# A third place for split weights, modulation loads of the wide projections dealt into two halves, gathers shared by two engines

## The chip, the cores and the metric

The kernel runs on one core of one Trainium2 chip. The engines are TensorE (PE, matrix products; PEld is its weight load), VectorE (DVE), ScalarE (ACT), GpSimd (POOL) and SyncE (SP), whose queue issues the DMA loads. All run on their own and are tied by semaphores; each does its instructions in strict order. The metric is the time of one execution in microseconds (us), lower is better.

## The reference

Two blocks of a network run over 256 tokens of width 2048, all in float32. The part that fixes the work, cut:

```python
def first_block(...):
    h = rmsnorm(x); proj = h @ w_in                 # 2048 x 5120
    x = x + concat([pool_mixer(u), hgrn2(q, f, i, g)]) @ w_out
    x = x + memory_cross_attention(h, m, wq, wk, wv, wo)   # four 2048 x 2048
    x = x + hierarchical_moe(h, ...)                # 16 experts, width 512, top 1 group, top 2 in it
...
def second_block(x, c, ...):
    c_act = jax.nn.silu(c)
    for l in range(2):
        mod = c_act @ w_ada[l] + b_ada[l]           # 2048 x 6144
        shift, scale, gate = jnp.split(mod, 3, axis=-1)
        h = _rmsnorm(x, norm_g[l]) * (1.0 + scale) + shift
        z = h @ w_in[l]                             # 2048 x 6656, 13 pieces
        o_fft = _fourier_mix(f_x, w_fft[l]) * silu(f_g)
        o_na = _neighbourhood_attention(na_q, na_k, na_v, ...) * silu(na_g)
        o_ret = _retention(r_q, r_k, r_v, ...) * silu(r_g)
        o_cv = _conformer_conv(cv_a, cv_b, ..., w_pw[l]) * silu(cv_g)
        x = x + gate * (concat([o_fft, o_na, o_ret, o_cv]) @ w_out[l])
```

## The kernel before, in words

**Weight blocks.** All large weights are read in blocks of 128 x 2048 float32 (1 MB). SyncE loads each into a raw room (`load`, L471); the rooms are dealt by `raw_rooms`: four outside the experts, more in them. ACT writes 256 times the block as float16 (`w_hi`, L644), DVE what is left over, raw times 256 minus the high half (`w_lo`, L1292, in `split`), and thereby gives the room back (`raw_taken`). There are two places for the halves (`SPL`), so ACT's work on a block waits until PE is done with the block two back (`block_done`). PE makes 48 products of a block (`product`, L2241): high weights with high and low activations, low weights with the high ones. It waits for the split of its own block (`taken`).

**Stages.** `w_in` (40 blocks), `w_out`, `wk`, `wq`, `wv`, `wo` (16 each), `moe` (192 blocks in a larger ring), then for each layer `z0`/`z1` (the wide projection, 52 blocks) and `mix0`/`mix1` (16). In the experts, tokens are first gathered by matmuls into 16 pieces (L2556, L2670 follows); ACT evicts the high half of each (`gather_hi`), DVE the low half (`gather_lo`, L1867).

**Modulation.** The product with `w_ada` (12 units of 16 steps) is done on the side. A step is a load of 0.5 MB (`load_ada`, L476) into one of two staging halves and one operation on DVE, sum plus weights times a column (`ada_step`, L1263), which stands right behind the split of its block. `ada_plan` lists the block of each step. SyncE issues the load of block m, then the modulation loads of block m - 2 (`load_due(2)`), and each of these waits until the step two back is done (`ada_used`). A unit ends with small products on PE (`ada_columns`) and an addition (`ada_add`). Units 7 and 8 run in z0, 10 and 11 in z1, all in blocks 2 to 29, with staging and sums in `Z` (`Z_UNITS`).

**Beside the wide projection.** Its 13 pieces come in `Z_ORDER`; attention, retention, Fourier mixing and convolution are written between blocks at fixed numbers. `TAPS_AT` deals the 124 taps of the convolution to blocks. After block 43 SyncE loads `w_fft` into a raw room, after block 48 `conv_w_pw`. The room of `w_fft` is given back by PE itself, at the last product of `fft_map` (L2818), which stands ahead of block 45. DVE has `conv_norm` (L2068 to L2071) and `mixed_lo` (L2124) between the splits of blocks 44 and 45.

The order of all this is written out by hand in each engine's program; no scheduler changes it.

Of the kernel before, what the change touches and what calls it, by code (L numbers as in the profile page):

```python
# [24 lines left out]
SPL = 2  # L25
# [24 lines left out]
Z_UNITS = (7, 8, 10, 11)  # L50
# [4 lines left out]
TAPS_AT = {**{m: 4 for m in range(11, 20)}, 20: 6, 21: 3, 22: 5, 23: 6, 24: 3, 25: 5, 26: 6, 27: 3, 28: 3, 29: 6, 30: 2,  # L55
           31: 6, 32: 2, 33: 6, 34: 3, 35: 4, 36: 4, 37: 4, 38: 7}
# [140 lines left out]
def build(nc, A, table, const_at, columns, router, out):  # L197
    ctx = ExitStack()
    with ctx:
# [21 lines left out]
        w_hi = sb("w_hi", [P, SPL, BLK], F16)  # L221
        w_lo = sb("w_lo", [P, SPL, BLK], F16)
# [65 lines left out]
        f_parts = w2[:, 0:1024].rearrange("p (a k g n) -> p a k g n", a=TT, k=2, g=4)  # L288
        f_last = w2[:, 1024:1032].rearrange("p (a g) -> p a g", a=TT)
# [8 lines left out]
        LO_AT = {"ga": 0, "weight": KC, "t": KC + 1, "y": KC + 1 + 4 * TILES}  # L298
# [77 lines left out]
        def ada_bank(u):  # L376
            return MB[:, 0, 0:8] if u in (8, 11) else GB[:, 2, 0:8]
# [77 lines left out]
        def _(sp):  # L455
# [26 lines left out]
            def load_due(depth):

                while len(due) > depth:
# [136 lines left out]
        def _(act):  # L621
            def split_half(ph, j, half):
# [7 lines left out]
                act.activation(w_hi[:, s % SPL, cut], raw_at[r][:, cut], ACT.Copy, scale=W_SCALE).then_inc(hi_done, 1)  # L630

            def split(ph, j, i=0):
# [3 lines left out]
                if ph == "moe":  # L636
                    act.wait_ge(block_done[s % SPL], s // SPL - 1)
# [375 lines left out]
            for n in range(MOE_STEPS):  # L1013
                f, last = n // 8, n % 8 == 7
                for part in range(2):
# [19 lines left out]
                    if n == 2 and part == 1:  # L1035
# [205 lines left out]
        def _(dve):  # L1241
# [23 lines left out]
            def ada_add(u):  # L1265
                dve.wait_ge(ada_mm, u + 1)
                mod = MOD[:, u // 6, u % 6 * 8:u % 6 * 8 + 8]
                if u % 6 < 4:
# [5 lines left out]
                    ("z0", 20): 7, ("z0", 33): 8, ("mix0", 14): 9, ("z1", 20): 10, ("z1", 33): 11}  # L1274

            def split_half(ph, j, half):
# [1717 lines left out]
```

## Time and profile before

| | us |
|---|---|
| median of three runs | 2095.44 |
| lowest, highest | 2094.69, 2101.43 |
| profiled execution | 2093.71 |
| its span | 2091.7 |
| outside the span | 2.0 |

The mean clock granted to PE is 0.994 of full. The stages in the profiled execution, by PE's work: w_in to 265.5, w_out to 353.2, wk to 439.6, wq to 533.8, wv to 629.7, wo to 724.7, experts 738 to 1233, z0 1248.5 to 1572.8, mix0 to 1660.1, z1 1668.0 to 1994.0, mix1 to 2077.7. Times in the timelines are counted from the span's start. The waits view adds up the idle time of an engine under what ended it, so a wait for several things stands under the last one.

### The profile page before, as it was taken

How to read it: one execution, taken by the hardware profiler on the slowest of the kernel's cores; microseconds unless marked ns; L12 is line 12 of the kernel's file. 1: busy time of each engine (PE TensorE's matmuls, PEld its weight loads, DVE VectorE, ACT ScalarE, POOL GpSimd, SP SyncE). 2: the span in 40 equal slices, each digit the busy share in tenths (PEclk: the TensorE clock that was granted, in tenths of full speed). 3: DMA queues.
4: the chain of work that ended last, by engine and by line, in shares of the span. 5: the costliest groups of instructions: out<-in, count | busy, mean ns of one | idle time of the engine just before them, and what ended most of it. 6: DMA issues, size and time to landing. Idle time of an engine off the chain costs nothing.

```text
span 2091.7 us, 42599 instructions
## 1 busy us (share of the span) xinstructions
PE 2041.4 (98%) x18993; PEld 1641.1 (78%) x18993; DVE 1752.3 (84%) x1670; ACT 1194.1 (57%) x1071; POOL 41.3 (2%) x40
## 2 busy tenths in 40 slices
PE   8999999999999989999999999999999899999998
PEld 7889888888889946555556568888888788888887
DVE  7875787988888799999999999999668779996555
ACT  5554644444445478877877864456554444565543
POOL 0002300000000000000000000000000000000000
PEclk9999999999999999999999999999999999999999
DMA  8854487789888878999999987874458778744452
GB/s 303 317 202 162 163 314 271 280 307 326 319 326 298 309 280 355 420 420 420 420 420 416 408 318 293 294 256 164 143 184 310 281 286 304 250 162 159 181 202 101
DMA packets 95717, 593.23 MB, mean 284 GB/s; under 512 B 10664, under 2 KB 10824, under 8 KB 36784
## 3 DMA queue, kind: packets, MB, share of 16 engines
q1 hardware_dynamic: 94912, 583.73, 74.4%
q0 software_dynamic: 624, 6.80, 0.8%
q8 instruction: 149, 2.44, 0.5%
q14 instruction: 32, 0.26, 0.0%
HBM read 588.39 MB, written 2.10 MB: 282 GB/s over the span
## 4 chain that ended last, share of the span: by engine, by line
PE 68%; DVE 16%; DMA 10%; ACT 3%; issue 3%; DVEq 0%; SPq 0%; POOL 0%; ACTq 0%; POOLq 0%
PE GB L2241 52%; DVE w_lo L1292 6%; PE GB L2670 4%; DVE W L1292 3%; PE MB L2670 3%; DMA raw<-w_up 3%; DMA W<-w_ada 2%; ACT w_hi L644 2%; DMA Z<-w_ada 2%; DMA raw<-w_down 2%; DVE W L1263 1%; DVE Z L1263 1%; DMA raw<-w_gate 1%; PE MB L2839 1%; PE MB L2441 1%
## 5 line engine op out<-in xcount | busy, mean ns | idle before, releaser
L644 ACT ACTIVATE w_hi<-raw 128x2048 f16<-128x2048 f32 x308 | 588.1, 1910 | 705.5 <-PE GB L2241 680.9
L1292 DVE SCALAR_TENSOR_TENSOR w_lo<-raw,w_hi 128x2048 f16<-128x2048 f32 x308 | 706.0, 2294 | 244.9 <-ACT w_hi L644 244.2
L2241 PE MATMUL GB<-H,w_hi 128*128 128x256 f16 x4352 | 718.9, 273 | 18.3 <-DVE w_lo L1292 11.6
L2241 PE MATMUL GB<-H,w_lo 128*128 128x256 f16 x2176 | 593.8, 273 | 0.0
L2241 PEld LDWEIGHTS GB<-H,w_hi 128*128 128x128 f16 x4352 | 421.6, 98 | 85.0 <-DVE w_lo L1292 16.6
L2241 PEld LDWEIGHTS GB<-H,w_lo 128*128 128x128 f16 x2176 | 213.2, 98 | 24.9
L2241 PE MATMUL GB<-w_hi,H 128*128 128x256 f16 x1280 | 210.7, 273 | 0.0
L1263 DVE SCALAR_TENSOR_TENSOR W<-W,SM 128x1024 f32<-128x1024 f32 x120 | 153.8, 1282 | 31.8 <-DMA W<-w_ada 28.5
L2241 PE MATMUL GB<-w_lo,H 128*128 128x256 f16 x640 | 174.4, 273 | 0.0
L2241 PE MATMUL GB<-Z,w_hi 128*128 128x256 f16 x1024 | 170.0, 274 | 2.9 <-DVE w_lo L1292 2.9
L2241 PE MATMUL GB<-W,w_hi 128*128 128x256 f16 x1024 | 168.0, 273 | 2.7 <-DVE w_lo L1292 2.7
L2241 PE MATMUL GB<-Z,w_lo 128*128 128x256 f16 x512 | 140.4, 274 | 0.0
L2241 PE MATMUL GB<-W,w_lo 128*128 128x256 f16 x512 | 139.6, 273 | 0.0
L2241 PEld LDWEIGHTS GB<-w_hi,H 128*128 128x128 f16 x1280 | 124.7, 98 | 16.1 <-issue 1.3
L1292 DVE SCALAR_TENSOR_TENSOR W<-raw,W 128x2048 f16<-128x2048 f32 x54 | 123.2, 2286 | 2.3 <-ACT W L644 2.2
L644 ACT ACTIVATE W<-raw 128x2048 f16<-128x2048 f32 x54 | 103.0, 1911 | 20.9 <-DMA raw<-w_down 6.1
L2241 PEld LDWEIGHTS GB<-Z,w_hi 128*128 128x128 f16 x1024 | 100.4, 98 | 16.0 <-DVE w_lo L1292 3.8
L2241 PEld LDWEIGHTS GB<-W,w_hi 128*128 128x128 f16 x1024 | 99.9, 98 | 14.9 <-DVE w_lo L1292 3.3
L2008 DVE SCALAR_TENSOR_TENSOR Y<-Y,PC 128x256 f32<-128x256 f32 x240 | 99.6, 479 | 0.0
L2670 PE MATMUL GB<-W,Z 128*64 (+1 forms) x864 | 86.7, 353 | 4.4 <-DVE Z L1867 4.3
L2670 PE MATMUL MB<-W,Z 128*64 (+1 forms) x864 | 86.0, 353 | 1.3 <-DVE W L1292 1.2
L1263 DVE SCALAR_TENSOR_TENSOR Z<-Z,SM 128x1024 f32<-128x1024 f32 x60 | 76.8, 1281 | 10.7 <-DMA Z<-w_ada 9.9
(489 smaller groups left out, 2789.9 us busy)
## 6 DMA issues: line engine op xcount, KB each, us to landing
raw<-w_in SPq DMA_DIRECT2D x144, 1024.0 KB, 5.2
W<-w_ada SPq DMA_DIRECT2D x128, 512.0 KB, 5.6
raw<-w_out SPq DMA_DIRECT2D x48, 1024.0 KB, 5.1
raw<-w_down SPq DMA_DIRECT2D x41, 1024.0 KB, 10.6
raw<-w_gate SPq DMA_DIRECT2D x34, 1024.0 KB, 11.0
raw<-w_up SPq DMA_DIRECT2D x32, 1024.0 KB, 12.8
Z<-w_ada SPq DMA_DIRECT2D x64, 512.0 KB, 5.9
raw<-xattn_wk SPq DMA_DIRECT2D x16, 1024.0 KB, 5.1
```

What stands on the lines that cost most here:

```text
L644: act.activation(w, raw_at[r], ACT.Copy, scale=W_SCALE).then_inc(hi_done, 1)
L1263: dve.scalar_tensor_tensor(sums, w, SM[:, 24 + k:25 + k], sums, ALU.mult, ALU.add).then_inc(ada_used[n % 2], 1)
L1292: dve.scalar_tensor_tensor(lo, raw_at[r], W_SCALE, hi, ALU.mult, ALU.subtract).then_inc(raw_taken[r], 1)
L2008: dve.scalar_tensor_tensor(ca[:, c, :], CU[:, c, k // 4:k // 4 + T], col("conv_w_2", l * TAPS * 4 + k), ca[:, c, :], ALU.mult, ALU.add).th ...
L2241: last = pe.matmul(o, a, m, start=first, stop=end and w_part is lo, skip_group_check=True)
L2441: ins = pe.matmul(MB[:, h % 2, a * T:a * T + T], x_q[q][:, 4 * h + c, a * P:a * P + P], x_k[k][:, 4 * h + c, :], start=a == 0 and c == 0 a ...
L2670: ins = pe.matmul(o_bank(j, k)[r:r + SLOT], x[:, c0 + c, at_:at_ + SLOT], v, start=kh == 0 and c == 0 and part == 0, stop=kh == 7 and c == ...
L2839: ins = pe.matmul(banks[:, n // 2, n % 2 * T:n % 2 * T + T], w[:, k, n * P:n * P + P], x[:, k, :], start=n % 2 == 0 and k == 0, stop=k == ...
```

## The change

- `SPL` is 3. Two places stay as they were; the third is the fourth raw room, cut into a high and a low half (`third`, `hi_of`, `lo_of`). Block s uses place `(s + 2) % 3`. ACT waits for the block three back.
- Three raw rooms are left outside the experts; the fourth joins the ring there from the experts' fifth block, and the wide projection gets it back as a place.
- The gathers' low half of odd pieces goes from DVE to ACT.
- `ada_plan`: in z0 and z1 the first unit stands in blocks 2 to 16, the second in blocks 35 to 46 and is staged in `W` instead of `Z`; its first load waits for the attention's output (`na_o`, `LATE_ROOM`). Its columns are at block 50, its addition at 51.
- `TAPS_AT` deals the same 124 taps anew. `f_parts` and `f_last` move from `w2` to `w1`. In the experts the router's steps, `best_two`, `place_rows` and an exponential stand one to three steps later.

```diff
-SPL = 2
+SPL = 3
-Z_UNITS = (7, 8, 10, 11)
+Z_UNITS = (7, 10)
...
-TAPS_AT = {**{m: 4 for m in range(11, 20)}, 20: 6, 21: 3, 22: 5, 23: 6, 24: 3, 25: 5, 26: 6, 27: 3, 28: 3, 29: 6, 30: 2,
-           31: 6, 32: 2, 33: 6, 34: 3, 35: 4, 36: 4, 37: 4, 38: 7}
+TAPS_AT = {11: 5, 12: 4, 13: 6, 14: 4, 15: 6, 16: 4, 17: 6, 18: 6, 19: 6, 20: 6, 21: 6, 22: 2, 23: 6, 24: 6, 25: 2, 26: 6, 27: 6, 28: 2, 29: 4, 30: 6, 32: 6, 33: 2, 34: 6, 35: 2, 36: 3, 37: 2}
...
-        open_ = list(range(RAW))
+        open_ = list(range(RAW - 1))
         if 0 <= j < n:
-            open_ += [4] * (j >= 6) + [5] * (7 <= j < 126) + [6] * (j >= 7) + [7] * (13 <= j < 150)
+            open_ += [3] * (j >= 4) + [4] * (j >= 6) + [5] * (7 <= j < 126) + [6] * (j >= 7) + [7] * (13 <= j < 150)
...
-    def fast(ph):
-        for m in [2 + 2 * k // 3 for k in range(13)] + list(range(11, 30)):
+    def halves(ph):
+        for m in [2, 2, 3, 4, 4, 5, 6, 6, 7, 8, 8, 9, 10, 12, 14, 16]:
+            put(ph, m)
+        for m in [35, 36, 37, 37, 38, 39, 39, 40, 41, 41, 42, 42, 43, 44, 45, 46]:
             put(ph, m)
...
+        third = raw[:, RAW - 1, :].bitcast(F16)
+        hi_of = [w_hi[:, 0, :], w_hi[:, 1, :], third[:, 0:BLK]]
+        lo_of = [w_lo[:, 0, :], w_lo[:, 1, :], third[:, BLK:2 * BLK]]
+
+        def slot(s):
+
+            return (s + 2) % SPL
...
-                    act.wait_ge(block_done[s % SPL], s // SPL + 2 * i)
-                    w = w_hi[:, s % SPL, :]
+                    act.wait_ge(block_done[s % SPL], s // SPL)
+                    if (ph, j) == ("z0", 0):
+                        given_up(act, RAW - 1)
+                    w = hi_of[slot(s)]
...
             def gather_hi(c):
                 act.wait_ge(S("moe_mm"), MM_AT["ga"] + c + 1)
+                if c % 2:
+                    act.activation(xs_lo[:, c, :], gather_bank(c, 1), ACT.Copy)
...
             def gather_lo(c):
-                dve.wait_ge(S("moe_mm"), MM_AT["ga"] + c + 1)
-                dve.tensor_copy(xs_lo[:, c, :], gather_bank(c, 1)).then_inc(S("moe_lo"), 1)
+                if c % 2 == 0:
+                    dve.wait_ge(S("moe_mm"), MM_AT["ga"] + c + 1)
+                    dve.tensor_copy(xs_lo[:, c, :], gather_bank(c, 1)).then_inc(S("moe_lo"), 1)
...
-                    if m == 17:
+                    if m == 19:
                         ada_columns(7 + 3 * l)
-                    if m == 32:
-                        pe.wait_ge(S("na_max"), 8 * l + 8)
+                    if m == 50:
+                        pe.wait_ge(S("fft_act"), 7 * l + 7)
                         ada_columns(8 + 3 * l)
```

What stands in SyncE's order in z0 around the load of `w_fft`, before. `raw_taken` with a number is the room that the load waits for, `raw<-w_in` the weight block; the last four are blocks 44, 45, 46 and 47:

```order
L471 DMA raw<-w_in 128x2048 [waits raw_taken3]
L471 DMA raw<-w_fft 128x2048 [waits raw_taken0]
L536 DMA NYQ<-w_nyq 4x512
L471 DMA raw<-w_in 128x2048 [waits raw_taken1]
L471 DMA raw<-w_in 128x2048 [waits raw_taken2]
L471 DMA raw<-w_in 128x2048 [waits raw_taken3]
L471 DMA raw<-w_in 128x2048 [waits raw_taken0]
```

Now, from the same place; the weight blocks are 44, 45, 46 and `ada_used` is the staging half that a modulation load waits for:

```order
L482 DMA raw<-w_fft 128x2048 [waits raw_taken0]
L550 DMA NYQ<-w_nyq 4x512
L482 DMA raw<-w_in 128x2048 [waits raw_taken1]
L487 DMA W<-w_ada 128x1024 [waits ada_used0]
L487 DMA W<-w_ada 128x1024 [waits ada_used1]
L482 DMA raw<-w_in 128x2048 [waits raw_taken2]
L487 DMA W<-w_ada 128x1024 [waits ada_used0]
L482 DMA raw<-w_in 128x2048 [waits raw_taken0]
L487 DMA W<-w_ada 128x1024 [waits ada_used1]
```

The room of `w_fft` is asked for again by block 46's load instead of block 47's, and two modulation loads stand ahead of block 45's, one ahead of and one behind block 46's.

DVE's order in z0 from the split of block 44, before (`hi_done` is ACT's high half, `mix_hi` its part of the mixed output):

```order
L1292 SCALAR_TENSOR_TENSOR w_lo<-raw,w_hi 128x2048 [waits hi_done]
L2068 RECIPROCAL NS<-NS 128x256 [waits conv_dve,conv_act]
L2069 TENSOR_TENSOR Y<-Y,NS 128x1024 [waits dve_step]
L2071 TENSOR_SCALAR Y<-Y,PC 128x256 [waits dve_step]
L2071 TENSOR_SCALAR Y<-Y,PC 128x256 x3
L2124 TENSOR_TENSOR W<-Y,W 128x1024 [waits mix_hi]
L1292 SCALAR_TENSOR_TENSOR w_lo<-raw,w_hi 128x2048 [waits hi_done] x2
```

Now, from the same split to the split of block 45 and the modulation step behind it:

```order
L1310 SCALAR_TENSOR_TENSOR w_lo<-raw,w_hi 128x2048 [waits hi_done]
L1281 SCALAR_TENSOR_TENSOR W<-W,SM 128x1024 [waits ada_used0,ada_full1]
L2087 RECIPROCAL NS<-NS 128x256 [waits conv_dve,conv_act]
L2088 TENSOR_TENSOR Y<-Y,NS 128x1024 [waits dve_step]
L2090 TENSOR_SCALAR Y<-Y,PC 128x256 [waits dve_step]
L2090 TENSOR_SCALAR Y<-Y,PC 128x256 x3
L2143 TENSOR_TENSOR W<-Y,W 128x1024 [waits mix_hi]
L1310 SCALAR_TENSOR_TENSOR raw<-raw 128x2048 [waits hi_done]
L1281 SCALAR_TENSOR_TENSOR W<-W,SM 128x1024 [waits ada_used1,ada_full0]
```

A modulation step stands behind each of the two splits, the first ahead of `conv_norm`, and the split of block 45 writes its low half into the fourth raw room.

## Rows read from the trace of the kernel before

**Rows 1.** The page's first part: busy us of each engine, share of the span, instructions.

```profile
PE 2041.4 (98%) x18993; PEld 1641.1 (78%) x18993; DVE 1752.3 (84%) x1670; ACT 1194.1 (57%) x1071; POOL 41.3 (2%) x40
```

**Rows 2.** Table by stage: length, busy of PE, PEld, DVE, ACT, POOL, clock, DMA share, GB/s.

```profile
738.10:1233.00 494.90, 482.89 (x4845) 274.76 (x4846) 472.66 (x297) 399.95 (x276) 0.00 (x0) 1.00 0.98 396
1248.50:1572.80 324.30, 320.26 (x2814) 274.33 (x2815) 279.43 (x345) 169.40 (x193) 0.00 (x0) 1.00 0.63 225
1668.00:1994.00 326.00, 320.35 (x2812) 273.89 (x2813) 273.28 (x329) 169.39 (x193) 0.00 (x0) 1.00 0.63 225
```

**Rows 3.** Waits of PE: engine and line, waited for what; us in total, times, longest.

```profile
PE GB L2241 <- DVE w_lo L1292: 17.3, 20, 2.1
PE GB L2670 <- DVE Z L1867: 5.2, 5, 1.6
```

**Rows 4.** The same view, waits of DVE.

```profile
DVE w_lo L1292 <- ACT w_hi L644: 246.0, 167, 9.6
DVE W L1263 <- DMA W<-w_ada: 28.5, 33, 1.8
```

**Rows 5.** Timeline of SyncE's queue in z0: start us, us, engine, line, operation, tiles.

```profile
1491.65 37.99 SPq L471 DMA_DIRECT2D raw<-w_in  x5
```

**Rows 6.** Waits of SyncE's queue, 1480 to 1540.

```profile
SPq L471 <- PE GB L2818: 22.9, 1, 22.9
```

**Rows 7.** Timeline of DVE in z0, blocks 41 to 45.

```profile
1491.55 1.22 DVE L2055 SCALAR_TENSOR_TENSOR Z<-MB,Z 128x1024 f32<-128x1024 f32 x1
...
1500.30 0.68 DVE L1995 TENSOR_TENSOR Z<-Y 128x512 f32<-128x512 f32 x1
1501.02 0.42 DVE L1996 TENSOR_TENSOR Z<-Z 128x256 f32<-128x256 f32 x1
...
1505.54 0.42 DVE L2059 COPY Z<-GB 128x256 f32<-128x256 f32 x1
...
1508.26 1.23 DVE L2102 TENSOR_TENSOR raw<-raw 128x1024 f32<-128x1024 f32 x1
1512.21 2.29 DVE L1292 SCALAR_TENSOR_TENSOR w_lo<-raw,w_hi 128x2048 f16<-128x2048 f32 x1 [2.73 <-ACT w_hi L644]
1514.42 1.75 DVE L2068 RECIPROCAL NS<-NS 128x256 f32<-128x256 f32 x1
...
1519.89 2.28 DVE L1292 SCALAR_TENSOR_TENSOR w_lo<-raw,w_hi 128x2048 f16<-128x2048 f32 x1
```

**Rows 8.** Timeline of PE in z0: retention, then the starts of blocks 43, 44, 45.

```profile
1489.62 1.08 PE L2765 MATMUL GB<-Z 128*64 128x256 f32 x8
...
1510.44 0.38 PE L2241 MATMUL GB<-H,w_hi 128*128 128x256 f16 x2
...
1515.68 0.38 PE L2241 MATMUL GB<-H,w_hi 128*128 128x256 f16 x2
...
1528.96 0.38 PE L2241 MATMUL GB<-H,w_hi 128*128 128x256 f16 x2
```

**Rows 9.** Timeline of SyncE's queue in w_out: a weight load and the modulation load behind.

```profile
300.12 0.33 SPq L471 DMA_DIRECT2D raw<-w_out  x1
300.50 0.43 SPq L476 DMA_DIRECT2D W<-w_ada  x1
```

**Rows 10.** Modulation loads (L476), 300 to 325: issue to landing.

```profile
DMA to landing us min/median/max: 5.9/6.3/6.8
```

**Rows 11.** The same line, 1390 to 1405.

```profile
DMA to landing us min/median/max: 5.2/5.3/5.4
```

**Rows 12.** The page's fifth part: busy us, mean ns, idle before; a modulation step on DVE.

```profile
L1263 DVE SCALAR_TENSOR_TENSOR W<-W,SM 128x1024 f32<-128x1024 f32 x120 | 153.8, 1282 | 31.8 <-DMA W<-w_ada 28.5
```

**Rows 13.** Table of stretches, columns as in rows 2: two blocks of w_in, and pre-experts.

```profile
38.17:45.09 6.92, 6.92 (x48) 5.49 (x49) 6.38 (x5) 1.27 (x3) 0.00 (x0) 0.75 0.99 374
45.09:50.33 5.24, 5.24 (x50) 4.70 (x48) 3.04 (x2) 2.40 (x2) 0.00 (x0) 1.00 0.98 392
728.11:734.94 6.83, 6.79 (x36) 6.08 (x35) 5.60 (x32) 3.72 (x7) 0.00 (x0) 0.50 0.87 367
```

More of the change, by code:

```diff
@@ L165, in ada_plan @@
         put("wo", m)
-    fast("z0")
+    halves("z0")
     for m in [2, 2, 3, 4, 4, 5, 6, 6, 7, 8, 8, 9, 9, 10, 10, 11]:
         put("mix0", m)
-    fast("z1")
+    halves("z1")
     assert count[0] == 12 * ADA_STEPS
@@ L220, in build @@
         raw = sb("raw", [P, RAW, BLK])
-        w_hi = sb("w_hi", [P, SPL, BLK], F16)
-        w_lo = sb("w_lo", [P, SPL, BLK], F16)
+        w_hi = sb("w_hi", [P, 2, BLK], F16)
+        w_lo = sb("w_lo", [P, 2, BLK], F16)
         XT = sb("XT", [P, KC, T])
@@ L287, in build @@
         RO = Y[:, 5:7, :]
-        f_parts = w2[:, 0:1024].rearrange("p (a k g n) -> p a k g n", a=TT, k=2, g=4)
-        f_last = w2[:, 1024:1032].rearrange("p (a g) -> p a g", a=TT)
+        f_parts = w1[:, 0:1024].rearrange("p (a k g n) -> p a k g n", a=TT, k=2, g=4)
+        f_last = w1[:, 1024:1032].rearrange("p (a g) -> p a g", a=TT)
         f_cos, f_nyq, f_sin = Zf[:, 0:2 * MIRROR], Zf[0:4, 2 * MIRROR:3 * MIRROR], Zf[:, 2 * T:2 * T + 2 * MIRROR]
@@ L297, in build @@
         HI_AT = {"ga": 0, "pt": KC, "t": KC + 3, "y": KC + 3 + 4 * TILES}
-        LO_AT = {"ga": 0, "weight": KC, "t": KC + 1, "y": KC + 1 + 4 * TILES}
+        LO_AT = {"ga": 0, "weight": KC // 2, "t": KC // 2 + 1, "y": KC // 2 + 1 + 4 * TILES}
         SQ_AT = {"x": 0, "wo": 4, "two": 12, "mix0": 18, "mix1": 26}
@@ L361, in ada_sums @@
             if u in Z_UNITS:
-                return Zf[:, (4 * (u in (8, 11))) * T:(4 * (u in (8, 11)) + 4) * T]
+                return Zf[:, 0:4 * T]
             return SUMS[:, u % 2, :]
@@ L376, in ada_bank @@
         def ada_bank(u):
-            return MB[:, 0, 0:8] if u in (8, 11) else GB[:, 2, 0:8]
+            return MB[:, 0, 0:8] if u in Z_UNITS else GB[:, 2, 0:8]
         def na_p(h):
@@ L418, in piece_end, with done @@
             return 2 + u if i == 0 and ph in K_MAJOR else 4 * i + 2 * u + 1
-        def done(eng, ph, j, i=0):
+        def done(eng, ph, j):
             s = where(ph, j)[1]
-            eng.wait_ge(block_done[s % SPL], s // SPL + 1 + 2 * i)
+            eng.wait_ge(block_done[s % SPL], s // SPL + 1)
         def pieces_in(eng, k):
@@ L464, in load @@
                     sp.wait_ge(raw_taken[r], n - 1)
+                elif r == RAW - 1:
+                    done(sp, "wo", 13)
                 elif r == 4:
@@ L478, in _ @@
             ADA_ROOM = {"w_out": ("hgrn_y", 2), "z0": ("norm_ms", 4), "mix0": ("small_mm", 2), "z1": ("norm_ms", 5)}
+            LATE_ROOM = {8 * ADA_STEPS: 4, 11 * ADA_STEPS: 8}
             due = []
@@ L488, in load_due @@
                     for step in steps:
+                        if step in LATE_ROOM:
+                            sp.wait_ge(S("na_o"), LATE_ROOM[step])
                         load_ada(step)
@@ L629, in split_half @@
                 cut = slice(half * BLK // 2, half * BLK // 2 + BLK // 2)
-                act.activation(w_hi[:, s % SPL, cut], raw_at[r][:, cut], ACT.Copy, scale=W_SCALE).then_inc(hi_done, 1)
+                act.activation(hi_of[slot(s)][:, cut], raw_at[r][:, cut], ACT.Copy, scale=W_SCALE).then_inc(hi_done, 1)
             def split(ph, j, i=0):
@@ L636, in split @@
                 if ph == "moe":
-                    act.wait_ge(block_done[s % SPL], s // SPL - 1)
+                    act.wait_ge(block_done[(s - 4) % SPL], (s - 4) // SPL + 1)
                     if j < 2:
@@ L1034, in _ @@
                             turned_hi(n // 16 - 1, k)
-                    if n == 2 and part == 1:
+                    if n == 3 and part == 1:
                         act.wait_ge(S("r_exp_in"), 1)
@@ L1273, in _ @@
             adds = {("w_in", 22): 0, ("wk", 10): 1, ("wq", 9): 2, ("wv", 3): 3, ("wv", 13): 4, ("wo", 8): 5,
-                    ("z0", 20): 7, ("z0", 33): 8, ("mix0", 14): 9, ("z1", 20): 10, ("z1", 33): 11}
+                    ("z0", 20): 7, ("z0", 51): 8, ("mix0", 14): 9, ("z1", 20): 10, ("z1", 51): 11}
             def split_half(ph, j, half):
@@ L1280, in split_half @@
                 cut = slice(half * BLK // 2, half * BLK // 2 + BLK // 2)
-                ins = dve.scalar_tensor_tensor(w_lo[:, s % SPL, cut], raw_at[rooms[b][0]][:, cut], W_SCALE, w_hi[:, s % SPL, cut], ALU.mult, ALU.subtract)
+                ins = dve.scalar_tensor_tensor(lo_of[slot(s)][:, cut], raw_at[rooms[b][0]][:, cut], W_SCALE, hi_of[slot(s)][:, cut], ALU.mult, ALU.subtract)
                 if half:
@@ L1926, in _ @@
                     if part == 1:
-                        if n == 0:
+                        if n == 2:
                             groups_left()
-                        if n == 2:
+                        if n == 3:
                             best_two()
@@ L1932, in _ @@
                             combine()
-                        if n in (3, 4):
-                            place_rows(n - 3)
+                        if n in (4, 6):
+                            place_rows(n // 2 - 2)
                     if n == 6 and part == 1:
@@ L2224, in product @@
                 s = at[ph][1] + j
-                hi = w_hi[:, s % SPL, :].rearrange("p (c n) -> p c n", c=8)
-                lo = w_lo[:, s % SPL, :].rearrange("p (c n) -> p c n", c=8)
+                hi = hi_of[slot(s)].rearrange("p (c n) -> p c n", c=8)
+                lo = lo_of[slot(s)].rearrange("p (c n) -> p c n", c=8)
                 first = start
@@ L2702, in na_scores @@
                         evicted(pe, l, 3)
+                        pe.wait_ge(ada_mod, 8 + 3 * l)
                     else:
@@ L2736, in rotate @@
                     if j == 0:
-                        pe.wait_ge(ada_mod, 8 + 3 * l)
+                        pe.wait_ge(ada_mod, 7 + 3 * l)
                     else:
```

9 lines of the change are left out of this document (4 added, 5 removed).

## The prediction

> **What bounds the kernel now.** The page's first part is read first: TensorE (PE) is busy 2041.4 of the 2091.7 us of the span [rows 1]. A change pays only where PE stands still. The table by stage says where that is [rows 2]: in z0 and z1 all but 4 to 6 us are matmuls, and only the mixture of experts (first row) is tied to DMA, at a share of 0.98. PE's waits are the second view: 17.3 us in 20 waits for the low half of a weight block (longest 2.1) and 5.2 us in the gathers, the first two lines of a list that falls off fast [rows 3]. So a third place has at most some 17 us to win outside the experts, and halved gathers about 5. Third view, VectorE's (DVE) waits: 246.0 us in 167 for the high half, 28.5 in 33 for modulation loads, the longest 1.8 [rows 4]. DVE has slack, but its order is fixed, so a late modulation load stops all that is queued behind it, splits included.
>
> **The dangerous place: w_fft.** In each wide projection SyncE loads w_fft after block 43, into a raw room of the ring. That room isn't given back by a DVE split but by PE: `fft_map`'s last matmul, ahead of block 45. Before, SyncE waited 22.9 us for it [rows 6], within the five loads that run from 1491.65 to 1529.64 [rows 5]. That was harmless: with four rooms the load that waited was that of block 47, blocks 44 to 46 were out already, and no modulation load stood behind it. The change makes it three rooms and puts steps of unit 8 there. The order of SyncE shows that now block 46's load waits for the room, and behind it, on a queue in strict order, the modulation load that DVE wants in block 44, since modulation loads are issued two blocks late. DVE has that step ahead of `conv_norm`, `mixed_lo` and the split of block 45; PE can't begin block 45 without that split. The load thus starts when PE is already idle, and three engines take turns.
>
> **Times at that place, layer 0.** First X, from the end of a split (a room comes free) to the landing of a modulation load that is queued behind the weight load. The two are issued 0.4 us apart [rows 9]; the second lands 5.9 to 6.8, median 6.3, after its issue [rows 10]. X = 0.4 + 6.3 = 6.7 us. Lower bound: elsewhere it lands 5.2 to 5.4 after its issue [rows 11], 0.4 + 5.2 = 5.6. But there it was issued 1.2 us behind the weight load and so had less ahead of it; the value of the close pairs is the nearer one. Upper bound, with the longest landing: 7.2.
>
> The Trainium skill, "DMA: Bandwidth & Descriptors", section "Anatomy of one DMA — SWDGE (gpsimd) path", gives about 2.0 us and bytes/436e9 for one transfer. For 1.5 MB that is an estimate of 5.6 us, with the 0.4 between the issues 6.0 instead of 6.7; it would take 0.7 off each of six terms, 4.2 us. It speaks of GpSimd's path, these are SyncE's, and the landings above contradict it, so the rows decide.
>
> Now the chain. DVE split block 44 at 1512.21 and block 45 at 1519.89 [rows 7]; PE reached block 43 at 1510.44 and block 44 at 1515.68, so the split of block 44 was over 1.2 us ahead, that of block 45 long before [rows 8]. In the new order block 44's load waits for the split of block 42, with the two modulation loads of block 42 behind it. DVE's three operations on retention's first scores (from 1491.55, 2.7 us) can begin when PE has these at 1490.6 [rows 8]; the split of block 42, 2.3, follows them: 1495.6, if its load is there. Then:
> - the first of the two lands at 1495.6 + 6.7 = 1502.3, the second 1.3 later; a step takes 1.28 us [rows 12], so both are over at 1504.9. With 1.1 for the convolution's squares (0.68 and 0.42, rows 7) and the split (2.29), block 43 is ready at 1508.3. PE wants it at 1510.44: no wait.
> - block 45's load waits for this split, the next modulation load lands at 1508.3 + 6.7 = 1515.0, its step ends at 1516.3. Then come the copy and the three tensor operations that stood at 1505.54 to 1509.45 (3.9), and the split (2.3): block 44 is ready at 1522.5. PE wants it at 1515.68: **wait of 6.9 us**.
> - PE does block 44 and `fft_map`, whose last matmul before the change ended at about 1528.9, and block 45 started at 1528.96, a wait of under 0.1 [rows 8]. Call that end T0. Now T0 + 6.7 is the landing, + 1.3 the step, + 5.5 `conv_norm` and `mixed_lo` (1514.42 to 1519.89, rows 7), + 2.3 the split = T0 + 15.8: **wait of 15.7 us**.
>
> Nothing covers these: PE has the 24 matmuls of `fft_map` and nothing else ahead of block 45. Together 22.6 us a layer. Layer 1 has the same order and almost the same figures (320.35 against 320.26 us of matmuls [rows 2]), so **+45.2 us**. Bounds: with X at 5.6, 3.3 less a layer (it enters three times), so −6.6; at 7.2, 0.5 six times, +3.0.
>
> **The clock.** After a wait of some 2 us that ended at 38.17 (one of those in rows 3), the granted clock of PE is 0.75 on average over a block, which takes 6.92 us, the next 5.24 at 1.00 [rows 13]: 1.7 us. The levels are 1.2 and 2.4 GHz, so it was at the lower for about half. After a longer pause ahead of the experts it was 0.50 for all of 6.83 us, which costs 3.4. Four long waits at 1.7 each: **+6.8** (bounds 0, if no fall follows, and 13.6).
>
> **The gathers.** ScalarE (ACT) takes the low half of odd pieces, DVE half as many copies; PE's waits there are 5.2 us [rows 3]. In this stretch ACT has time. The experts then run with DMA, which is full behind them: what the gathers give comes through only as far as loads were not the limit. I take **−4** (bounds −5 and 0).
>
> **The third place and the halves.** ACT's split no longer waits for the block two back but three back. Gain: part of the 17.3 us, at most −9, since those waits at the start of w_in (2.1 among them) are loads and norm work that a place doesn't make earlier. Loss: one raw room fewer means that load and modulation loads are released one block later. Two consecutive blocks with three steps between them need of DVE's chain X + 1.3 + 1.3 + 2.3 = 11.6 us, against 10.5 for PE's two blocks; there are 14 such pairs (4 in w_in, 3 in z0, 4 in mix0, 3 in z1), each up to 1.1 us less the lead built up, at most +12. I take **0** net, the middle of −9 and +12. The convolution's taps dealt into other blocks are the same instructions: the busiest blocks now have 6 and no step, as some had before; cover is DVE's own wait for the high half [rows 4]. 0. The steps of unit 8, which leave blocks 11 to 29, relieve SyncE and DVE where PE didn't wait anyway. In the experts, `groups_left`, `best_two`, the exponential and `place_rows` come one to two steps later, work of a few us in total whose reader, the gathers, is far off: 0. `ada_columns` of unit 8 at block 51 is 16 small matmuls as before: 0.
>
> **Sum.** 2093.7 (profiled execution, 2.0 us above its span) + 45.2 + 6.8 − 4 + 0 = 2141.7. The median of the runs is 1.7 above the profiled execution: **2143 us**, 2.3% slower.
>
> **Rivals.**
> - **The lead covers it (faster).** One mechanism: at w_fft the modulation load of block 44 is out before `fft_map` ends. It decides if the load is issued 15.8 us ahead of T0. Then the waits of the low half (17.3), some of them, and of the gathers go, and DVE has freer blocks 11 to 29: −20, about 2075. For it: DVE waits 246 us on ACT, so slack is plenty [rows 4]. Against: the printed order leaves SyncE no way past the room's release. Chance 0.03.
> - **Only the weight load is late.** If DVE had its step of block 44 from elsewhere, block 46 alone hangs on T0: landing 4.8, ACT 1.9, DVE 2.3 are 9.0, against 5.24 of block 45, wait 3.7. Twice, with 3.4 for the clock and −4 for the gathers: 2095.4 + 7.4 + 3.4 − 4 = 2102. It is also what remains if DVE's work between is overlapped by something that I overlook. Chance 0.05.
> - **Pairs with three steps fall behind too.** The deficits of the 14 pairs open in full, +12: 2155. For it: DVE waited already 28.5 us for such loads with a room more [rows 4]. Chance 0.15.
> - **It doesn't do what it says** (PE reaches block 44 later than thought, by waits earlier in the stage, so that its wait of 6.9 shrinks; the sum moves along with the last rival). It's inside the forecast's range.
>
> **How the numbers follow.** The forecast has 0.77. Low end: no clock loss −6.8, X at its lower bound −6.6, and 7.6 of the 9 that the places may gain: 2122. High end: clock +6.8, X +3.0, pairs +11: 2164. This leaves out the two cheap rivals (0.08) and some tail. A measurement of this kernel can tell 0.3%, 6.3 us, from no change; the forecast and the third rival are slower beyond it (0.92), the second rival (+6.6) lies at the bound and I split it evenly, 0.025 and 0.025. Faster 0.03, same 0.03, slower 0.94.
>
> **What would show it.** In the changed kernel: a wait of SyncE for `fft_map` that now has block 46's load behind it; DVE's longest waits for a modulation load (over 5 us) right after the split of blocks 43 and 44; two PE waits for a low half in each of z0 and z1, near 7 and 16 us, the second directly behind `fft_map`; a granted clock of 0.50 after them; PE's waits in the gathers near 0. A wait of under 4 us behind `fft_map` would make the forecast wrong, and a wait for modulation loads in w_in or mix0 of over 1 us a block would speak for the third rival.

## The result and the profile after

The changed kernel takes 2205.52 us (median of 4, 2202.47 to 2207.54) against 2095.07 before: a ratio of 1.0519, 95% interval 1.0495 to 1.0543. The forecast was 2143 us, slower by 2.3%; it is slower by 5.2%, and outside the range of 2122 to 2164. The direction and one mechanism were right, the size wasn't.

The page's first part of the changed kernel, which answers to rows 1:

```profile
span 2205.7 us, 42602 instructions
PE 2066.4 (94%) x18993; PEld 1647.7 (75%) x18993; DVE 1751.9 (79%) x1662; ACT 1196.7 (54%) x1079; POOL 42.4 (2%) x40
```

The work is the same: DVE is busy 1751.9 us, before 1752.3. PE's busy time grew by 25 of the 114 us, with the same instructions at a lower granted clock (0.977 on average, before 0.994); the rest is PE standing still. For what, its list of waits says (changed kernel; us in total, times, longest):

```profile
PE GB L2260 <- DVE w_lo L1310: 76.3, 41, 15.1
PE GB L2260 <- DVE raw L1310: 28.9, 14, 16.0
PE MB L2689 <- DVE W L1310: 4.0, 4, 2.1
```

Both first lines are the low half of a weight block (`raw` is the third place, cut from the fourth raw room): 105 us in 55 waits, where rows 3 had 17.3 in 20. DVE in turn waits for modulation loads, where rows 4 had 28.5 in 33 (and the same list 9.9 in 9 for those in `Z`):

```profile
DVE W L1281 <- DMA W<-w_ada: 203.3, 86, 22.7
DVE w_lo L1310 <- ACT w_hi L660: 82.2, 61, 6.8
DVE Z L1281 <- DMA Z<-w_ada: 31.2, 20, 3.3
DVE raw L1310 <- ACT raw L660: 23.6, 12, 9.0
```

DVE's waits for the high half fell from 246.0 to 82.2 + 23.6 us, and reappear as waits for loads of `w_ada`. A table of stages, worked out from PE's first and last product of each stage in the traces, tells where the time went (us longer than before; one profiled execution of each kernel; "w_in to wo" is the sum of its six stages; "w_fft" is from the start of block 42 to that of block 47, both layers together, and is taken out of z0 and z1):

| kernel | w_in to wo | experts | z0 + z1 without w_fft | w_fft | mix0 |
|---|---|---|---|---|---|
| changed | 34.4 | −1.8 | 12.6 | 61.2 | 6.1 |
| third place alone | 25.2 | 2.2 | 26.6 | 12.6 | 6.1 |
| three rooms, two places | 33.1 | 1.9 | 24.0 | 11.5 | 4.8 |
| new plan and taps alone | 0.5 | 0.8 | −4.0 | 13.6 | 1.9 |
| changed, nearer loads | −6.6 | 2.3 | −4.2 | 13.1 | −2.4 |
| changed, three late steps | 28.9 | 1.2 | 21.6 | 38.6 | 6.0 |

So over half of the loss (61.2) is at the place that the prediction named, priced there at 45.2 and 6.8 for the clock. Another 53 us are in the dense stages, for which it had put down 0.

**At w_fft.** SyncE's queue from the end of block 43's split on, and then DVE from block 44's split on, changed kernel, z0 (start us, us, engine, line, operation, tiles; in brackets idle time and what ended it):

```profile
1553.70 0.33 SPq L482 DMA_DIRECT2D raw<-w_in  x1
1554.07 0.43 SPq L487 DMA_DIRECT2D W<-w_ada  x1
1584.30 0.33 SPq L482 DMA_DIRECT2D raw<-w_in  x1
1584.67 0.43 SPq L487 DMA_DIRECT2D W<-w_ada  x1
```

```profile
1566.31 2.28 DVE L1310 SCALAR_TENSOR_TENSOR w_lo<-raw,w_hi 128x2048 f16<-128x2048 f32 x1
1591.25 1.29 DVE L1281 SCALAR_TENSOR_TENSOR W<-W,SM 128x1024 f32<-128x1024 f32 x1 [22.66 <-DMA W<-w_ada]
1592.46 1.75 DVE L2087 RECIPROCAL NS<-NS 128x256 f32<-128x256 f32 x1
1594.24 1.23 DVE L2088 TENSOR_TENSOR Y<-Y,NS 128x1024 f32<-128x1024 f32 x1
1595.50 1.38 DVE L2090 TENSOR_SCALAR Y<-Y,PC 128x256 f32<-128x256 f32 x4
1596.80 1.22 DVE L2143 TENSOR_TENSOR W<-Y,W 128x1024 f16<-128x1024 f32 x1
1597.93 2.28 DVE L1310 SCALAR_TENSOR_TENSOR raw<-raw 128x2048 f16<-128x2048 f32 x1
```

Between the second and the third of SyncE's lines it waited for `fft_map`'s last product (waits of SyncE's queue, 1540 to 1610):

```profile
SPq L482 <- PE GB L2837: 29.8, 1, 29.8
```

It issued block 46's load at 1584.30. The modulation load behind it landed 6.9 us later (1591.23); step, `conv_norm`, `mixed_lo` and split ended at 1600.21, 15.9 after T0 (predicted 15.8). The waits of PE there:

```profile
PE GB L2260 <- DVE raw L1310: 16.0, 1, 16.0
PE GB L2260 <- DVE w_lo L1310: 10.6, 2, 9.5
```

16.0 us at block 45 (predicted 15.7), 9.5 at block 44 (6.9) and 1.1 at block 43 (0). In z1 they are 15.1, 6.9 and 1.5. The clock, by stretches (columns as in rows 2; blocks 44, 45, 46):

```profile
1568.65:1576.26 7.61, 7.61 (x47) 5.86 (x48) 0.00 (x0) 0.14 (x1) 0.00 (x0) 0.67 0.00 0
1600.27:1607.44 7.17, 7.17 (x47) 5.63 (x48) 4.31 (x3) 0.59 (x1) 0.00 (x0) 0.71 0.88 330
1607.55:1612.68 5.13, 5.13 (x49) 4.61 (x47) 4.98 (x5) 3.83 (x4) 0.00 (x0) 1.00 0.23 61
```

A block behind a long wait takes 7.6 or 7.2 us instead of 5.1 to 5.2, granted 0.67 and 0.71 on average: 4.5 us in this layer (predicted 3.4).

**In the dense stages.** The same in small, in w_in, where there is no w_fft. SyncE and DVE of the changed kernel, blocks 7 to 9:

```profile
62.13 0.33 SPq L482 DMA_DIRECT2D raw<-w_in  x1
62.50 3.42 SPq L487 DMA_DIRECT2D W<-w_ada  x2
```

```profile
59.82 2.28 DVE L1310 SCALAR_TENSOR_TENSOR w_lo<-raw,w_hi 128x2048 f16<-128x2048 f32 x1
64.28 1.28 DVE L1281 SCALAR_TENSOR_TENSOR W<-W,SM 128x1024 f32<-128x1024 f32 x1 [2.18 <-DMA W<-w_ada]
65.48 2.29 DVE L1310 SCALAR_TENSOR_TENSOR w_lo<-raw,w_hi 128x2048 f16<-128x2048 f32 x1
69.68 2.67 DVE L1281 SCALAR_TENSOR_TENSOR W<-W,SM 128x1024 f32<-128x1024 f32 x2 [1.91 <-DMA W<-w_ada]
...
73.53 2.29 DVE L1310 SCALAR_TENSOR_TENSOR raw<-raw 128x2048 f16<-128x2048 f32 x1
```

The split of block 7 ends at 62.10 and frees the room for block 10's load (62.13); the modulation loads of block 8 stand behind that; the first lands at 69.66. Two steps, 1.2 us of small operations for HGRN's decay (left out above), and block 9's split ends at 75.82. From split to split, two blocks on, 13.7 us, while PE needs 10.5 for two blocks. PE began block 9 at 75.88, right behind it, after a wait of 2.6 us, and took 6.61 us for it at a mean granted clock of 0.79.

### The profile page after: what moved, and what is told of

Read it like the earlier page. It is cut to its first block, busy times and chain, and to the rows that moved or that the text cites. A ratio compares the mean times of both kernels' runs of the same rounds, so it can differ in the third digit from the quotient of the medians.

```text
span 2205.7 us, 42602 instructions
## 1 busy us (share of the span) xinstructions
PE 2066.4 (94%) x18993; PEld 1647.7 (75%) x18993; DVE 1751.9 (79%) x1662; ACT 1196.7 (54%) x1079; POOL 42.4 (2%) x40
## 4 chain that ended last, share of the span: by engine, by line
PE 25%; DVE 24%; issue 24%; DMA 23%; ACT 3%; SPq 1%; POOLq 0%; DVEq 0%; POOL 0%; ACTq 0%
DMA W<-w_ada 15%; PE GB L2260 12%; DVE w_lo L1310 8%; DVE W L1281 5%; PE GB L2689 4%; PE MB L2689 4%; DMA raw<-w_up 3%; DVE raw L1310 3%; DVE W L1310 2%; DMA Z<-w_ada 2%; ACT w_hi L660 2%; DMA raw<-w_gate 1%; DMA raw<-w_down 1%; SPq L482 1%; DMA Y<-mem 1%
## 5 line engine op out<-in xcount | busy, mean ns | idle before, releaser
L1310 DVE SCALAR_TENSOR_TENSOR w_lo<-raw,w_hi 128x2048 f16<-128x2048 f32 x223 | 511.1, 2295 | 81.4 <-ACT w_hi L660 80.6
L660 ACT ACTIVATE w_hi<-raw 128x2048 f16<-128x2048 f32 x223 | 425.0, 1906 | 208.7 <-PE GB L2260 116.0
L2260 PE MATMUL GB<-H,w_hi 128*128 128x256 f16 x2880 | 485.1, 276 | 52.0 <-DVE w_lo L1310 51.2
L2260 PE MATMUL GB<-H,w_lo 128*128 128x256 f16 x1440 | 396.6, 275 | 0.0
L1281 DVE SCALAR_TENSOR_TENSOR W<-W,SM 128x1024 f32<-128x1024 f32 x150 | 192.5, 1283 | 208.0 <-DMA W<-w_ada 203.3
L2260 PEld LDWEIGHTS GB<-H,w_hi 128*128 128x128 f16 x2880 | 281.0, 99 | 99.9 <-DVE w_lo L1310 58.0
L2260 PE MATMUL GB<-H,raw 128*128 128x256 f16 x2208 | 254.7, 276 | 30.4 <-DVE raw L1310 26.1
L2260 PEld LDWEIGHTS GB<-H,raw 128*128 128x128 f16 x2208 | 216.3, 99 | 65.6 <-DVE raw L1310 29.4
L1310 DVE SCALAR_TENSOR_TENSOR raw<-raw 128x2048 f16<-128x2048 f32 x85 | 195.3, 2298 | 23.9 <-ACT raw L660 23.6
L660 ACT ACTIVATE raw<-raw 128x2048 f16<-128x2048 f32 x85 | 161.9, 1905 | 94.1 <-PE GB L2260 49.1
L2260 PEld LDWEIGHTS GB<-H,w_lo 128*128 128x128 f16 x1440 | 142.5, 99 | 17.8
L1101 ACT ACTIVATE Z<-GB 128x512 f32<-128x512 f32 x44 | 26.2, 596 | 139.2 <-PE GB L2260 139.1
## 6 DMA issues: line engine op xcount, KB each, us to landing
raw<-w_down SPq DMA_DIRECT2D x41, 1024.0 KB, 10.6
raw<-w_gate SPq DMA_DIRECT2D x34, 1024.0 KB, 11.6
raw<-w_up SPq DMA_DIRECT2D x32, 1024.0 KB, 13.1
```

The lines of the kernel that those rows point to most:

```text
L660: act.activation(w, raw_at[r], ACT.Copy, scale=W_SCALE).then_inc(hi_done, 1)
L1101: act.activation(Z[:, 4 * n + 2 * u:4 * n + 2 * u + 2, :], GB[:, u, :].rearrange("p (c t) -> p c t", t=T), f, scale=INV).then_inc(bank_fre ...
L1281: dve.scalar_tensor_tensor(sums, w, SM[:, 24 + k:25 + k], sums, ALU.mult, ALU.add).then_inc(ada_used[n % 2], 1)
L1310: dve.scalar_tensor_tensor(lo, raw_at[r], W_SCALE, hi, ALU.mult, ALU.subtract).then_inc(raw_taken[r], 1)
L2260: last = pe.matmul(o, a, m, start=first, stop=end and w_part is lo, skip_group_check=True)
```

## The experiments

Each ratio is to runs of the kernel before that were made beside that kernel; their median was 2094.95 to 2097.40 us.

**One part at a time.** Third place alone: `SPL`, the rooms, `hi_of` and `lo_of`, and the waits that follow from them, on the kernel before.

```diff
-SPL = 2
+SPL = 3
-        open_ = list(range(RAW))
+        open_ = list(range(RAW - 1))
...
+        third = raw[:, RAW - 1, :].bitcast(F16)
+        hi_of = [w_hi[:, 0, :], w_hi[:, 1, :], third[:, 0:BLK]]
```

> The kernel before with the third place alone: three places for the halves, the fourth raw room given up for it outside the experts. Old plan of the modulation steps, old taps, old gathers. Theory A (a raw room short: a modulation load is issued only when the split three blocks back is over, and DVE waits for it with the next split behind it): the losses of the dense stages come with this edit alone. From the changed kernel's starts of blocks that is 34.5 us in w_in to wo, 6 in mix0, some 10 in z0 and 5 to 10 in z1; and block 46's load now waits for w_fft's room with no modulation step behind it, 3.7 a layer. Sum 60 to 65: about 2155 to 2160 us. Theory B (the new plan of steps is what costs, the room is harmless): within 8 us of before, 2090 to 2103.

Measured: 2167.21 us, ratio 1.0338 (1.0308 to 1.0368), 7 us above the upper end of theory A's numbers. 72 of the 110 us come with this edit.

Then the room taken away with nothing given for it:

```diff
-        open_ = list(range(RAW))
+        open_ = list(range(RAW - 1))
         if 0 <= j < n:
-            open_ += [4] * (j >= 6) + [5] * (7 <= j < 126) + [6] * (j >= 7) + [7] * (13 <= j < 150)
+            open_ += [3] * (j >= 4) + [4] * (j >= 6) + [5] * (7 <= j < 126) + [6] * (j >= 7) + [7] * (13 <= j < 150)
```

> The kernel before with three raw rooms instead of four outside the experts and nothing in exchange: two places, the fourth room lies idle there. Theory A: the same loss as with the third place or more, 2155 to 2175; the difference between this run and the one with the third place is what the place itself is worth, at most the 17 us that PE waited for low halves before. Theory B: within 8 us of before.

Measured: 2172.51 us, ratio 1.0373 (1.0344 to 1.0402). So it is the missing room and nothing about the place. DVE's waits in this kernel, where ACT has only two places and comes late to them, to be read against rows 4:

```profile
DVE w_lo L1292 <- ACT w_hi L644: 217.9, 119, 13.6
DVE W L1263 <- DMA W<-w_ada: 97.9, 64, 4.2
```

The plan of the modulation steps and the taps alone, on four rooms:

> The kernel before with the new plan of the modulation steps and the new taps alone: four raw rooms, two places, old gathers. Here block 47's load waits for w_fft's room as before, and the modulation load behind it is that of block 45. DVE has that step ahead of block 46's split: it lands 6.7 us after fft_map, the step takes 1.3, the split 2.3, together 10.3, and PE has only block 45's 5.2 in that time: a wait of some 5 us a layer, plus the clock. Theory A (order at w_fft is harmful only together with the missing room): 2095 + 10 + 3 = 2108, range 2100 to 2115. Theory B (the plan costs by itself): above 2130. If w_fft and the modulation steps do no harm at all: 2090 to 2097.

```diff
-Z_UNITS = (7, 8, 10, 11)
+Z_UNITS = (7, 10)
...
+        for m in [35, 36, 37, 37, 38, 39, 39, 40, 41, 41, 42, 42, 43, 44, 45, 46]:
             put(ph, m)
```

Measured: 2107.78 us, ratio 1.0065 (1.0048 to 1.0082), where theory A had 2108. The wait is at block 46, once in each layer. In z0, between 1500 and 1545:

```profile
PE GB L2245 <- DVE w_lo L1296: 5.2, 1, 5.2
```

5.2 us for 5 forecast, and 4.3 in z1. The table gives 13.6 us at w_fft for the plan on four rooms, 12.6 for the third place alone: 26.2 together. The remaining 35 of the 61.2 are an interaction, which neither edit has alone: only with both does the modulation step ahead of `conv_norm` hang on `fft_map`, and only with both is block 44 late, by 9.5 us.

The halved gathers and the router's later steps alone, without the rest of the change (cut to ACT's copy):

```diff
+                if c % 2:
+                    act.activation(xs_lo[:, c, :], gather_bank(c, 1), ACT.Copy)
```

> The kernel before with the halved gathers and the later router steps alone. PE waited 5.2 us for the low half in the gathers. Theory A: gain of 2 to 5 us, 2090 to 2093. Rival (the experts run with DMA, so a faster start is given back at the loads; or ScalarE's copies come late): no difference, 2095 plus or minus 1.

Measured: 2092.91 us, ratio 0.9993 (0.9979 to 1.0007). The interval goes from 4.4 us less to 1.5 more: not settled by the times. In the trace PE's waits there are 1.5 us for `gather_lo` and 1.6 for ACT, one each, where rows 3 had 5.2 in 5. The experts are 2.6 us shorter (1.8 in the changed kernel), but that is no measure of the edit: with the same gathers they are 2.3 and 1.2 us longer in the last two kernels of the table.

**The steps at w_fft.** The changed kernel with three steps of each layer's second unit moved back:

```diff
-        for m in [35, 36, 37, 37, 38, 39, 39, 40, 41, 41, 42, 42, 43, 44, 45, 46]:
+        for m in [35, 36, 37, 37, 38, 39, 39, 40, 41, 41, 42, 42, 43, 46, 46, 47]:
```

> The changed kernel with the modulation steps of blocks 44, 45, 46 put to 46, 46, 47, in both layers; all else as changed. Theory A: the wait of PE for block 45 (16.0 us) goes in each layer, since DVE has no step ahead of block 45's split; block 46's load still waits for w_fft's room, 3.7 and the clock's 1.7 to 2.5 at 46, and the two steps at 46 may make block 47 late by 2. The waits of block 43 and 44 (1.2 and 8 in layer 0) stay. So 2205 less 2 x (18 to 24) plus 2 x 7: 2170 to 2182. Theory B (the stall at w_fft comes from the room itself and not from the modulation load behind it): 2200 or more.

Measured: 2190.2 us, ratio 1.0441 (1.0408 to 1.0474): 15 us better, where 23 to 35 were expected. The wait of 16.0 at block 45 is gone, as theory A says, but others came behind it. PE's waits from 1540 to 1625; the first line is blocks 43, 44 and 46, the second block 48:

```profile
PE GB L2260 <- DVE w_lo L1310: 15.5, 3, 9.1
PE GB L2260 <- DVE raw L1310: 2.9, 1, 2.9
```

9.1 is block 44's, which the edit doesn't touch. At the release of the room SyncE issues the loads of blocks 46, 47 and 48 and the two modulation loads of block 46 in one go (1581.70 to 1584.22), so block 46, whose load started only now, is 5 us late. Block 48 is late by 2.9, since the step at 47 that stands ahead of its split has its load behind block 49's. From block 42 to 51 layer 0 lost 25.7 us against 31.7 in the changed kernel: moving the steps behind the release takes away the chain through `conv_norm`, not the loads' lateness. In the table the place itself gives back 22.6 us in both layers and the rest of z0 and z1 loses 9.0 more, so this run shows the part of one chain and doesn't account for all of the interaction.

**The distance of the loads.** The decisive run, one number in the changed kernel:

```diff
-                        load_due(2)
+                        load_due(1)
```

> The changed kernel with one number changed: SyncE issues the modulation loads of block m - 1, not m - 2, behind the weight load of block m. With three rooms that gives them the distance back (three blocks from the split that releases them) that they had with four rooms. Theory A: nearly all of the 35 us of w_in to wo, 6 of mix0 and some 9 and 4 of the first half of z0 and z1 come back; at w_fft block 44's modulation load is out ahead of the waiting load, so that what waits is block 46 with block 45's step: 10.3 less PE's 5.2, 5 a layer and the clock, as in the run with the plan alone (+5.4). 2205 - 54 - 62 + 14 = 2103, range 2095 to 2115. Theory B (DVE's own time, or PE's clock, is what costs in the dense stages): above 2150.

Measured: 2098.47 us, ratio 1.002 (1.0007 to 1.0033), so 107 of the 110 us are back (expected 2103, range 2095 to 2115). PE's waits for low halves fell from 105 us in 55 to 19 in 12, and DVE's for `w_ada` in `W` from 203.3 to 74.2:

```profile
PE GB L2260 <- DVE w_lo L1310: 11.4, 8, 5.2
PE GB L2260 <- DVE raw L1310: 7.5, 4, 4.3
```

The two longest are block 46 in z0 and z1, as with the plan alone. SyncE and DVE in it, at the place in w_in that was shown above:

```profile
55.49 0.43 SPq L482 DMA_DIRECT2D raw<-w_in  x1
56.51 3.93 SPq L487 DMA_DIRECT2D W<-w_ada  x2
60.48 0.43 SPq L482 DMA_DIRECT2D raw<-w_in  x1
```

```profile
59.99 2.29 DVE L1310 SCALAR_TENSOR_TENSOR w_lo<-raw,w_hi 128x2048 f16<-128x2048 f32 x1
62.54 1.28 DVE L1281 SCALAR_TENSOR_TENSOR W<-W,SM 128x1024 f32<-128x1024 f32 x1 [0.26 <-DMA W<-w_ada]
65.02 1.28 DVE L1281 SCALAR_TENSOR_TENSOR W<-W,SM 128x1024 f32<-128x1024 f32 x1 [1.19 <-DMA W<-w_ada]
...
67.47 2.29 DVE L1310 SCALAR_TENSOR_TENSOR raw<-raw 128x2048 f16<-128x2048 f32 x1
```

The modulation loads of block 8 (56.51) are now behind block 9's load (55.49), not block 10's (60.48), and the first is asked for ahead of block 8's split. DVE still waits 1.45 us for the two, yet block 9's split begins at 67.47, 6 us before its time in the changed kernel (1.1 of them lie at the start). The table has w_in to wo 6.6 us shorter than before the change.

The same number in the kernel before (`load_due(2)` to `load_due(1)`, nothing else):

> The kernel before with the same number changed, four rooms and two places. Theory A: DVE's waits for modulation loads (28.5 and 9.9 us) nearly vanish, and with them part of the 17.3 us that PE waited for low halves: 2083 to 2093. Rival: those waits were covered and PE's 17.3 come from something else: 2094 to 2096.

Measured: 2095.37 us, ratio 0.9997 (0.9985 to 1.0009): the rival is right. DVE's waits for `w_ada` in `W` went only from 28.5 to 24.8 us, PE's for low halves from 17.3 to 16.8. With four rooms the loads were early enough, and those waits of PE had another source. That the two places are part of it is shown below with three rooms; no run has four rooms and three places.

Then w_fft one block later, which changes the load that waits for its room from block 46's to block 47's:

```diff
-FFT_AFTER, PW_AFTER = 43, 48
+FFT_AFTER, PW_AFTER = 44, 48
```

> The changed kernel with the modulation loads one block nearer as in the run before the last, and w_fft loaded after block 44 instead of 43. Then it is block 47's load that waits for w_fft's room, with block 46's step behind it: ready 10.3 us after fft_map, when PE has blocks 45 and 46 (10.5) to do. Theory A: no wait at w_fft; 2103 less 14: 2089, range 2080 to 2097. If the room of w_fft isn't what makes these waits, as in the run with the nearer loads alone, 2100 to 2110.

Measured: 2090.29 us, ratio 0.9973 (0.9956 to 0.999). PE has no wait for a low half there any more; one for the pointwise weights is left, 1.7 us in each layer, since their load is the last in the queue behind the room. A further run loads `conv_w_pw` after block 47:

```diff
-FFT_AFTER, PW_AFTER = 44, 48
+FFT_AFTER, PW_AFTER = 44, 47
```

> The changed kernel with nearer modulation loads, w_fft after block 44 and conv_w_pw after block 47 instead of 48. In the run with w_fft after block 44 PE still waited 3.5 us in two waits for conv_w_pw and the clock fell behind them. Expected 2 to 4 us below that run: 2086 to 2088 where before is at 2095. If another wait takes its place: the same 2090.

Measured: 2084.95 us (5 runs, 2084.47 to 2086.47), ratio 0.9949 (0.9935 to 0.9962). It is a little below the 2086 to 2088 that were expected, and below both the kernel before and the changed one. What is left of PE's waits for low halves in it:

```profile
PE GB L2260 <- DVE w_lo L1310: 6.7, 6, 2.2
PE GB L2260 <- DVE raw L1310: 3.9, 3, 1.9
```

10.6 us in 9, with 17.3 in 20 before.

**What the place and the plan are worth once the loads are in time.** The kernels of the runs with the third place alone and with three rooms alone, each with the one line more:

```diff
-                        load_due(2)
+                        load_due(1)
```

> The kernel before with the third place (three raw rooms) and the modulation loads one block nearer; old plan, taps and gathers. Theory A: the dense stages lose nothing and may gain the 5 to 6 us that the changed kernel with nearer loads gained up to wv; block 46's load still waits for w_fft's room, 6.4 a layer with the clock as in the run with the place alone. 2095 + 13 - 5 = 2103, range 2098 to 2108. Rival (the old plan needs the fourth room in any case): above 2120.

> The same without the third place: three raw rooms, two places, the fourth room idle outside the experts, nearer modulation loads. The difference from the run with the place is what the place is worth once the loads are in time. Theory A: 2 to 6 us, so 2105 to 2109. Rival (a third place wins nothing, since DVE and not ACT is what a block waits for): the same as that run within 1 us.

Measured: 2099.19 us, ratio 1.001 (0.9999 to 1.0021), and 2109.27 us, ratio 1.0056 (1.0039 to 1.0073). The place is worth 10 us, more than the 2 to 6 that were expected. PE's waits for low halves, first with three places, then with two:

```profile
PE GB L2253 <- DVE w_lo L1304: 10.1, 8, 3.5
PE GB L2253 <- DVE raw L1304: 9.0, 6, 3.6
```

```profile
PE GB L2241 <- DVE w_lo L1292: 27.1, 22, 3.7
```

The 19.1 us in 14 and the 27.1 in 22 both hold about 7 us of waits at block 46, behind `w_fft`'s room. But a room for a place, with nearer loads and nothing else, only comes out even: 1.001 of before. What brings the kernels with `w_fft` after block 44 below before is the place together with the moved `w_fft` and the gathers. The kernel before with `w_fft` moved was not run, so it stays open what that alone is worth there; its trace has no wait of PE for a low half from 1520 to 1575, so there is little to win at that place.

Last, the kernel of 2084.95 us with the old plan of steps and the old taps:

```diff
-Z_UNITS = (7, 10)
+Z_UNITS = (7, 8, 10, 11)
...
+        for m in [2 + 2 * k // 3 for k in range(13)] + list(range(11, 30)):
             put(ph, m)
```

> As the run before, but with the old plan of the modulation steps and the old taps: third place, halved gathers, nearer loads, w_fft after 44, conv_w_pw after 47. It tells whether the second unit in blocks 35 to 46 is worth anything once nothing waits at w_fft. In the runs with nearer loads z1 was 2 us shorter before block 32 with the new plan. Expected 2 to 4 us above the run before: 2089 to 2092. Rival (the new plan is worth nothing): the same within 1 us.

Measured: 2084.57 us, ratio 0.9947 (0.9934 to 0.9961), the same as with the new plan. The rival is right: once nothing waits at w_fft, the second unit in blocks 35 to 46 is worth nothing that can be measured. In the changed kernel it was one half of the trap there, the missing room the other.

## Why the prediction was wrong, point by point

- **What bounds the kernel, the dangerous place, the chain at w_fft: right.** X was 6.9 us at 1584.30, for 6.7; at 1541.60 and 1553.70 it was 6.1 and 7.5, and the median of the changed kernel's 75 pairs issued so close is 6.3. By the page "DMA: Bandwidth & Descriptors" of the Trainium skill (section "Anatomy of one DMA — SWDGE (gpsimd) path") it would be 6.0, an estimate. The trace agrees with it no better than with the 6.7: the median lies between the two, and the wait that counts most had 6.9. The wait at block 45 was 16.0 for 15.7, that at block 44 9.5 for 6.9. The place cost 61.2 us in both layers, clock included, against 52.0. In layer 0 the 5 missing are 2.6 at block 44, 1.1 at block 43, 0.3 at block 45 and 1.1 of clock. The first two come mostly from the end of block 42's split. I had set it at the earliest moment that its inputs allow, 1495.6, and before the change PE began block 42 at 1504.75, 9 us later; in the new order it stood at 1541.58, only 5.3 us before PE wanted that block, with two steps and their loads to follow. About 0.8 of the 2.6 is X at block 44, 7.5.
- **The clock: right in kind**, 4.5 for 3.4 in z0 at w_fft. But it was counted only for four long waits. The many short waits in the dense stages also had slow blocks behind them, such as block 9 of w_in above, 6.61 us. PE's busy time grew by 10.4 us in the two stretches at w_fft and by 8.6 in w_in to wo, of 25 in all.
- **The gathers: −4.** The trace shows −1.8 in the experts and 1.5 us each left of PE's waits for the two copies, and alone the edit can't be told from nothing.
- **"The third place and the halves", 0 net: this step failed.** It was 53 us. Three things were wrong in it. First the count: it took only pairs of blocks that hold three steps, 14 of them in w_in, mix0 and the two wide projections, each at most 1.1 us short. But the chain (room free, weight load, modulation load behind it, steps of block m, split of block m + 1) runs from one split to the next but one, and by its own price of 11.6 it falls short wherever a block has two steps. Wq and wv alone have 20 such blocks, and the count left them out, with w_out, wk and wo. Second the price: it took the bare chain, and left out what else DVE does between the steps and the split. At blocks 7 to 9 the chain was 13.7, not 11.6: 1.2 of small operations, and 7.6 from the end of the split to the landing where the prediction had 6.7; why this landing was late is open. The slow blocks behind such waits had no term either. Third, it took "the lead built up" as a cover. With three rooms the load leaves only when the split just before it ends (62.13 behind 62.10), so a delay of DVE also delays the next load, and PE's waits go on through w_in: 2.6, 1.8 and 1.5 us at blocks 9, 11 and 13, where the kernel before has one, 1.3 at block 11. Rows 4's 28.5 us of waits at 1.8 at most said nothing of this chain: in the kernel before they stayed at 24.8 when the loads were brought nearer.
- **The rivals.** The third, that these deficits open, is what happened besides the forecast, but I had priced it at +12, where it was 53, and given it 0.15. Its price came from the same count. The rival "only the weight load is late" is what the third place alone shows at w_fft: one wait of 3.7 us at block 46 in each layer, for 3.7 in that rival's sum, and 6.3 a layer with the slow block behind it. The plan alone with four rooms and the changed kernel with nearer loads have 5.2 there in z0 and 4.3 in z1, with a modulation step in front of the split.
- **Range.** The upper end of 2164 rested on +12 as the bound of the room's cost. The same 1.1 us over every block with two steps (5 in w_in, 2 in w_out, 4 in wk, 20 in wq and wv, 6 in wo, 8 in the first halves of z0 and z1, 6 in mix0, together 51) would have been 56. That it comes so near 53 is in good part luck: w_in and w_out lost 15.1 us, where it gives 7.7, wq and wv 16.4 for 22, wk and wo 2.9 for 11.

## What to carry to other kernels

When a buffer is taken out of a ring, don't ask what the ring's own loads lose: list everything that stands behind those loads on the same queue, and count its distance, in blocks, from the release that starts it to the operation that needs it. If that distance is shorter than landing plus work on the way, every such round costs about the difference, and the next load starts late as well. Moving the small loads one block forward in the queue gave back 107 of 110 us here. And a release by the busiest engine (w_fft's room, given back ahead of block 45) must have no load behind it that this engine's next work needs.

## What I had not expected

Two edits that cost 72 and 13 us alone cost 110 together (with the gathers, which cost nothing), 25 more than their sum; at the place where they meet it is 61.2 against 26.2. And a kernel whose DVE idles a fifth of its span can be bound by DVE's order: busy time was 1752 us in the slowest and 1752 in the fastest of these kernels but one.
